# Attention in units of two heads, on even and odd query tokens

## The reference

```python
q_a, k_a, v_a, cx, cb, cc, q_m, gate_logits = split(rmsnorm(x) @ w_in)
# 12 attention heads of width 64: 3 groups x 4 slots
DIL_PATTERNS = ((128, 1), (512, 4), (2048, 16))   # (window, dilation) of a group
# query i attends the keys i + j*dilation with |j*dilation| <= window/2
s = where(valid, q . k / 8, -big)                  # inside each group
o_attn[slot] = sum over groups of softmax weights  # the groups are merged by their log-sum-exp
z_conv = cb * conv3(cc * cx)
# 4 memory heads of width 128 over 256 memory tokens
o_mem = softmax(q_m . k_m / sqrt(128)) @ v_m
x = x + (g0 * (o_attn @ w_proj_attn) + g1 * (z_conv @ w_proj_conv) + g2 * (o_mem @ w_proj_mem)) @ w_out
x = x + mixture_of_experts(rmsnorm(x))             # 32 experts, top 2 of one group of 8
```

## Time and profile before

| | |
|---|---|
| time, median of 3 runs | 2988.92 us (2987.07 to 2989.79) |
| span of the profiled execution | 2986.5 us, 2.4 us under the median |
| PE busy | 2817.0 us (94%) |
| DVE, ACT, POOL busy | 1155.4, 556.1, 621.8 us |
| chain that ended last | PE 86%, DMA 12%, DVE 1% |
| of that, slabs of the second block (L1561), experts' weights by DMA | 7%, 11% |
| attention stage, first scores to first `proj` | 2293.85 to 2459.64 us |

### The profile page before, as it was taken

How to read it: one execution, slowest core, us unless ns; L and a number is a source line. 1 busy time by engine, 2 the same in 40 slices (tenths; PEclk the granted TensorE clock), 3 DMA queues, 4 the chain that set the end, 5 groups by cost and what they waited for, 6 DMA issues and landing times.

```text
span 2986.5 us, 42182 instructions
## 1 busy us (share of the span) xinstructions
PE 2817.0 (94%) x18274; PEld 2423.2 (81%) x18274; DVE 1155.4 (39%) x2204; ACT 556.1 (19%) x856; POOL 621.8 (21%) x584
## 2 busy tenths in 40 slices
PE   8999999999999999999999999999999999866766
PEld 6888988889888899899988888889988888533433
DVE  3865235452433334745214344435355312210111
ACT  2101222124211101010033116210012330100000
POOL 0001411122121075068601210038800000000000
PEclk9999999999999999999999999999999999988878
DMA  9764543344443556764544444365433328899998
GB/s 406 297 263 163 175 150 134 121 141 171 140 141 127 196 199 229 272 219 166 183 147 143 139 153 143 130 224 170 165 135 130 105 91 351 381 432 430 430 430 371
DMA packets 74155, 641.62 MB, mean 215 GB/s; under 512 B 8304, under 2 KB 9584, under 8 KB 17648
## 3 DMA queue, kind: packets, MB, share of 16 engines
q1 hardware_dynamic: 71376, 631.55, 56.5%
q10 hardware_dynamic: 2592, 7.33, 0.6%
HBM read 637.80 MB, written 1.05 MB: 214 GB/s over the span
## 4 chain that ended last, share of the span: by engine, by line
PE 86%; DMA 12%; DVE 1%; issue 0%; ACT 0%; POOL 0%; SPq 0%; DVEq 0%; POOLq 0%; ACTq 0%
PE ps L1364 27%; PE ps L1340 20%; PE ps L1386 13%; DMA work<-in_w_moe 11%; PE ps L1561 7%; PE ps L1397 3%; PE ps L1591 2%; PE ps L1374 2%; PE ps L1145 2%; PE ps L1450 1%; PE ps L1167 1%; PE ps L1568 1%; PE ps L1272 1%; PE ps L1536 0%; PE ps L1539 0%; DMA ring<-in_w 0%
## 5 line engine op out<-in xcount | busy, mean ns | idle before, releaser
L2760 POOL TENSOR_TENSOR ring<-ring 128x512 f32<-128x512 f32 (+1 forms) x294 | 374.2, 1301 | 783.0 <-DMA ring<-in_w 315.7
L1364 PE MATMUL ps<-ring 128*128 128x256 f32 x2368 | 517.4, 380 | 0.6 <-ACT ring L1784 0.6
L1364 PEld LDWEIGHTS ps<-ring 128*128 128x128 f32 x2368 | 447.3, 190 | 63.2 <-issue 2.4
L2029 DVE TENSOR_TENSOR work<-work,ps 128x128 f32<-128x128 f32 (+3 forms) x534 | 185.6, 386 | 714.6 <-PE ps L1340 349.2
L1340 PE MATMUL ps<-work,ring 128*128 128x128 f32 x3312 | 385.8, 275 | 0.3 <-POOL work L2760 0.3
L1386 PE MATMUL ps<-work,ring 128*128 128x256 f32 x1760 | 385.5, 380 | 0.0
L1340 PEld LDWEIGHTS ps<-work,ring 128*128 128x128 f32 x3312 | 377.6, 192 | 0.5 <-POOL work L2760 0.5
L1386 PEld LDWEIGHTS ps<-work,ring 128*128 128x128 f32 x1760 | 332.5, 190 | 46.2 <-issue 2.1
L1364 PE MATMUL ps<-h,ring 128*128 128x256 f32 x1408 | 310.7, 382 | 6.5 <-ACT h L1784 2.9
L1364 PEld LDWEIGHTS ps<-h,ring 128*128 128x128 f32 x1408 | 265.8, 191 | 47.0 <-issue 5.7
L2029 DVE TENSOR_TENSOR work<-work 128x128 f32<-128x128 f32 (+4 forms) x566 | 261.6, 511 | 52.1 <-ACT eb L1812 24.9
(11 more groups left out here) (315 smaller groups left out, 2655.6 us busy)
## 6 DMA issues: line engine op xcount, KB each, us to landing
ring<-in_w SPq DMA_DIRECT2D x210, 1024.0 KB, 4.9
work<-in_w_moe SPq DMA_DIRECT2D x22, 4096.0 KB, 33.5
ring<-in_w_moe SPq DMA_DIRECT2D x22, 4096.0 KB, 33.4
ring<-in_w_in SPq DMA_DIRECT2D x80, 1024.0 KB, 4.9
work<-in_w_ada SPq DMA_DIRECT2D x40, 1024.0 KB, 6.1
ring<-in_w_ada SPq DMA_DIRECT2D x32, 1024.0 KB, 5.1
ring<-in_w SPq DMA_DIRECT2D x28, 768.0 KB, 4.2
ring<-in_w_out SPq DMA_DIRECT2D x16, 1024.0 KB, 5.1
```

What stands on the lines that cost most here:

```text
L1364: last = nc.tensor.matmul(ps[:, b, c * L:c * L + L], w[:, k * L + c * P:k * L + c * P + P], hs[cols][:, k, :], start=(k == 0), stop=(k == ...
L2029: return nc.vector.tensor_tensor(o, i0, i1, op)
L2760: return nc.gpsimd.tensor_tensor(o, i0, i1, ALU.subtract)
```

## The change

- There are 8 units, each with two neighbouring heads (`pair`). `t` is now a parity for form "a": even or odd query tokens (a stride of two in `q`, and in the normed `x` that is the stationary side of `va`, so that the values lie by parity too). Form "m" keeps its query tiles.
- Form "a", scores: the undilated group meets all 256 keys, the two dilated groups only the 128 of the query's parity. So a head's row of scores is 512 wide instead of 768. Head 0 of the pair uses array rows 0 to 63 and writes bank 4, head 1 uses rows 64 to 127 and writes bank 5.
- Maximum, sum and division are per head; ACT's exponential is two instructions of half the width.
- `turns`: 8 transposes ("a") or 4 ("m") and one wider copy. `mix`: 8 matmuls for "a", alternating between output rows 0 to 63 and 64 to 127, or 4 for "m". Its result goes to one of the four rotating banks; one ACT instruction copies both heads.
- Unit u has `scores` after slab 13 + 2u, `turns` after slab 14 + 2u, `mix` after slab 15 + 2u. The semaphore `un_out` is gone; `turns(u)` waits for the copy of the turns before (`un_pt`), and those who waited for 16 units wait for ACT's count after the last mix.
- Mask and `sc`, `pt` buffers are laid out for it.

```diff
-    for u in range(16):
-        side[u + 13].append(("scores", u))
-        side[u + 14].append(("turns", u))
-        side[u + 15].append(("mix", u))
+    for u in range(8):
+        side[2 * u + 13].append(("scores", u))
+        side[2 * u + 14].append(("turns", u))
+        side[2 * u + 15].append(("mix", u))
...
-        units = [("a", s, t) for s in range(4) for t in range(2)] + [("m", s, t) for s in range(4) for t in range(2)]
+        units = [(form, pair, t) for form in "am" for pair in range(2) for t in range(2)]
+        def parity(view, t):
+            return view.rearrange("p (u t) -> p t u", t=2)[:, t, :]
...
-                                last = nc.tensor.matmul(ps[:, b, t * L:t * L + L], hs[0][:, k, t * P:t * P + P],
+                                last = nc.tensor.matmul(ps[:, b, t * L:t * L + L], parity(hs[0][:, k, :], t),
...
                             for g in range(3):
-                                c = (g * 4 + slot) // 2
-                                last = nc.tensor.matmul(ps[:, 4 + g // 2, (g % 2) * L:(g % 2) * L + L],
-                                                        qk[r0:r0 + 64, c, t * P:t * P + P], qk[r0:r0 + 64, 6 + c, :],
-                                                        start=True, stop=True)
+                                c = 2 * g + pair
+                                for hh in range(2):
+                                    r = slice(64 * hh, 64 * hh + 64)
+                                    if g == 0:
+                                        dst, keys = ps[:, 4 + hh, 0:L].rearrange("p (t u) -> p t u", t=2), by_parity(qk[r, 6 + c, :])
+                                    else:
+                                        dst, keys = ps[:, 4 + hh, P + g * P:2 * P + g * P], parity(qk[r, 6 + c, :], t)
+                                    last = nc.tensor.matmul(dst, parity(qk[r, c, :], t), keys, start=True, stop=True,
+                                                            skip_group_check=True)
...
-                        nb = 6 if units[u][0] == "a" else 2
+                        nb = 8 if units[u][0] == "a" else 4
                         pe.wait_ge(un_pr, u + 1)
                         if u:
-                            pe.wait_ge(un_out, u)
+                            pe.wait_ge(un_pt, u)
...
+                        b = fresh()
...
+                            for j in range(4):
+                                g, tile = (0, j) if j < 2 else (j - 1, t)
+                                for hh in range(2):
+                                    hd = g * 4 + 2 * pair + hh
+                                    last = nc.tensor.matmul(ps[64 * hh:64 * hh + 64, b, 0:P], va[:, tile, hd * 64:hd * 64 + 64],
+                                                            pt[:, u % 2, hh * 512 + j * P:hh * 512 + j * P + P],
+                                                            start=(j == 0), stop=(j == 3), skip_group_check=True)
...
-                        nc.scalar.activation(sc[:, u % 2, 0:w], sc[:, u % 2, 0:w], ACT.Exp, bias=vms[:, u % 2:u % 2 + 1],
-                                             accum_out=vms[:, 2 + u % 2:3 + u % 2]).then_inc(un_ex, 1)
+                        for hh in range(2):
+                            last = nc.scalar.activation(sc[:, e, hh * w:hh * w + w], sc[:, e, hh * w:hh * w + w], ACT.Exp,
+                                                        bias=vms[:, 2 * e + hh:2 * e + hh + 1],
+                                                        accum_out=vms[:, 4 + 2 * e + hh:5 + 2 * e + hh])
+                        last.then_inc(un_ex, 1)
...
-                            nc.scalar.activation(oa[r, slot // 2, t * P:t * P + P], ps[r, 7, L:L + P], ACT.Copy
-                                                 ).then_inc(un_out, 1)
+                            nc.scalar.activation(parity(oa[:, pair, :], t), ps[:, b, 0:P], ACT.Copy).then_inc(ev_a, 1)
...
+                            own(stt(both, ps[:, 4:6, :], 64 ** -0.5, amask[:, t, :].unsqueeze(1).to_broadcast([P, 2, w]), mul, add))
...
+                        own(nc.vector.reciprocal(over, total))
+                        for hh in range(2):
+                            last = ts(sc[:, e, hh * w:hh * w + w], sc[:, e, hh * w:hh * w + w], over[:, hh:hh + 1], None, mul)
+                        last.then_inc(un_pr, 1)
```

More of the change, by code:

```diff
@@ L392, in __init__ @@
                 self.slabs += 1
-            if kind in ("gate", "up", "z", "wo", "mem", "msum", "xsum", "sum", "hsum", "in2", "proj", "out2") or (kind == "down" and stage[5] == 0):
+            if kind in ("gate", "up", "z", "wo", "mem", "msum", "xsum", "sum", "hsum", "in2", "mix", "proj", "out2") or (kind == "down" and stage[5] == 0):
                 assert groups < 4 or self.freed[groups - 4], (n, stage)
@@ L493, in __init__ @@
                 self.in2_at[stage[1:]] = self.a
+            elif kind == "mix":
+                self.a += 1
+                self.freed[self.group[n]] = ("a", self.a)
+                self.mixes_at = self.a
             elif kind == "hsum":
@@ L686, in build @@
         selw = shaped(mod[:].rearrange("p a b c -> p (a b c)")[0:N_EXP, 0:2 * P], 2, P)
-        sc = shaped(pmt[:, 0:2 * 3 * L], 2, 3 * L)
-        pt = shaped(glamask[:, 0:2 * 3 * L], 2, 3 * L)
+        sc = shaped(pmt[:], 2, 4 * L)
+        pt = shaped(glamask[:], 2, 4 * L)
         w_full = [sem(f"w_full{i}") for i in range(RING)]
@@ L1615, in first @@
                         u = stage[1]
-                        form, slot, t = units[u]
+                        form, pair, t = units[u]
                         if u == 0:
@@ L1649, in first @@
                         pe.wait_ge(un_pt, u + 1)
[L1650 to L1659, removed]
-                                                        xs[1][:, 4 + 2 * j + slot // 2, (slot % 2) * P:(slot % 2) * P + P],
-                                                        pt[:, u % 2, j * P:j * P + P], start=(j == 0), stop=(j == nb - 1))
+                        if form == "a":
+                            for j in range(4):
[5 more added lines that the diff above has]
+                                                            start=(j == 0), stop=(j == 3), skip_group_check=True)
+                        else:
+                            for hh in range(2):
+                                slot = 2 * pair + hh
+                                for j in range(2):
+                                    last = nc.tensor.matmul(ps[:, b, hh * P:hh * P + P],
+                                                            xs[1][:, 4 + 2 * j + slot // 2, (slot % 2) * P:(slot % 2) * P + P],
+                                                            pt[:, u % 2, hh * L + j * P:hh * L + j * P + P],
+                                                            start=(j == 0), stop=(j == 1), skip_group_check=True)
                         last.then_inc(un_o, 1)
@@ L1926, in first @@
                         u = stage[1]
[L1927 removed]
+                        form, pair, t = units[u]
+                        b = at.group[n] % 4
                         act.wait_ge(un_o, u + 1)
                         if form == "a":
[L1930 to L1934 removed]
+                            nc.scalar.activation(parity(oa[:, pair, :], t), ps[:, b, 0:P], ACT.Copy).then_inc(ev_a, 1)
+                        else:
+                            nc.scalar.activation(om[:, 2 * pair:2 * pair + 2, t * P:t * P + P],
+                                                 ps[:, b, 0:L].rearrange("p (s n) -> p s n", s=2), ACT.Copy).then_inc(ev_a, 1)
             act.dma_start(xs[1][:, :, :], a["ctx"]).then_inc(ctx_in, 16)
@@ L2522, in first @@
                         u = stage[1]
-                        form, slot, t = units[u]
+                        form, pair, t = units[u]
                         e = u % 2
-                        w = 3 * L if form == "a" else L
+                        w = 2 * L if form == "a" else L
                         if u == 0:
@@ L2848, in constants @@
         masks.append(np.where(ok, f(0), f(NEG)))
-    c["amask"] = np.ascontiguousarray(np.concatenate(masks, 1).astype(f).reshape(2, P, 3 * L).transpose(1, 0, 2))
+    near, fourth, sixteenth = masks
+    c["amask"] = np.stack([np.concatenate([near[t::2, 0::2], near[t::2, 1::2], fourth[t::2, t::2], sixteenth[t::2, t::2]], 1)
+                           for t in range(2)], 1).astype(f)
     c["desc"] = np.arange(8, 0, -1).astype(f)
```

39 lines of the change are left out of this document (20 added, 19 removed).

## The result

| | before | after |
|---|---|---|
| time, median | 2988.71 us (2987.07 to 2989.79, 4 runs) | 2969.51 us (2967.26 to 2970.20, 4 runs) |
| span of the profiled execution | 2986.5 us | 2965.7 us |
| first `scores` to first `proj` | 165.8 us | 146.1 us |
| first `proj` to the end | 526.9 us | 526.8 us |
| PE busy | 2817.0 us | 2796.8 us |

The ratio is 0.9933, 95% interval 0.9921 to 0.9945: the kernel is 19.2 us faster (forecast 20.2, time forecast 2968.7). Of the span's 20.8 us, 19.7 lie in the attention stage and 1.0 ahead of the first scores, where nothing was changed but the order of tokens in `va`. The stretch behind the stage is as long as before.

The account below looks back on a forecast made before the run. PE alone was taken to bound the attention stage, with later transfers started by PE. Attention on PE falls from 41.4 to 21.2 us (12.4 + 8.8), sparing 20.2: 2988.9 - 20.2 = 2968.7 us, range 2965.5 to 2976.5.

Parts of the forecast that it names:

- Rival (5): Experts' transfers start by something that didn't move, so spared time is not passed on: 2984 to 2989 us; chance 0.05.
- Scores "a": PE's scores block in four units: 1.06 us with two heads in row halves at once, 1.93 one after the other.
- Mix: PE's mix block of form "a": 16 passes in two column halves, 1.01 us, at worst 1.89.
- Transposes: PE's transposes block of form "a": 8 passes of 0.11 us plus 0.05, 0.93 us.
- Units "m": PE's four form "m" units: same products without the wait inside, 2.2 us each, 8.8 together, before 10.8.
- (1): Row halves don't overlap in scores, column halves in mix do: 3.5 us back, 2972.2 us; chance 0.10.
- (2): Neither scores' row halves nor mix's column halves overlap: 7.0 us back, 2975.7 us; chance 0.08.
- the variant with the loads in turn: Scores "a": the halves' weight loads go one after the other, 1.32 + 0.19 us; four units cost 1.8 us more.
- The chain: Softmax work between a unit's scores and transposes: 5.6 us, 5.8 with both ends; PE arrives after 6.91.
- Rival (3): PE waits at `turns` for a softmax of 8 us: 1 us in each of four units, 2972.7 us; chance 0.05.
- Strides: Queries, keys and `va` tokens read by PE with a stride of two floats: costed at nothing.
- Rival (4): Strided loads in `va` and scores "a" are slow: at f = 4, 3007.8 us; decides near f = 2.8; chance 0.04.

Follow-up runs that it names:

- x11: Changed kernel with both heads on the same array half and the parity-spared passes put back as repeats; stage 162.3 us against 146.1.
- x6: Changed kernel with the passes that the parity split spares put back as repeats, halves still side by side; stage 152.0 us, time 0.9955 of before.
- x3: Changed kernel with TensorE's operands read without the stride of two (output not the reference's); stage 145.9 us against 146.1.
- x10: Changed kernel with both heads of a form "a" pair on the same array half, same passes (output not the reference's); stage 153.3 us against 146.1.
- x7: Changed kernel with DVE's maximum of each form "a" unit taken twice; stage 146.1 us, as in the changed kernel.
- x8: Changed kernel with DVE's maximum of each form "a" unit taken four times; stage 158.8 us against 146.1, time 0.9979 of before.
- x4: Changed kernel with strided operands read at four floats instead of two (output not the reference's); stage 148.5 us against 146.1.

## Why the prediction was right

**PE bounds the stage and the rest follows it.** Right, and shown three ways: behind the stage it is 526.1 to 528.0 us in every kernel but x11, for stages from 146 to 159; x6 lost in the span what it lost in the stage; the first refill's issue moved by 20.7 us with the profile's 20.8, and from there to the end it is 434.2 us against 434.3. Rival (5) is out.

**The sum.** Forecast 21.2 us of attention on PE, measured 146.1 less 18 slabs of 6.91, 21.7: the stage is 0.5 us longer than forecast. Four terms make it up.

- Scores "a" were 1.13 instead of 1.06, 0.28 in four units; 0.05 of each 0.07 is the stride (x3 has 1.08).
- Mix was 1.01 forecast and 1.02 measured, 0.04 in all.
- Transposes took 0.87 instead of 0.93, 0.24 less in all. They now follow a slab, so no change of the array's form stands ahead of them.
- That change is paid elsewhere, and the forecast missed it. It counted one slab of 7.01 a unit, the one ahead of mix. Now a slab also stands directly behind the scores, and it takes 7.01 too: 0.4 in four units.

The trace of before shows this last cost in its first unit, the one whose scores have no transposes behind them (PE's timeline). The slab between two blocks of scores takes 7.10, with a change at both ends:

```profile
2295.34 7.17 PE L1561 MATMUL ps<-h,ring 128*128 128x256 f32 x32
2302.44 1.56 PE L1627 MATMUL ps<-work 64*128 64x256 f32 x6
```

Units "m" came to 0.89 + 0.87 + 0.44 = 2.2, as summed. The parts of the gain were given as 9 for scores left out, 7 for the halves and the rest (4.2) for fewer blocks; x11, x10 and the changed kernel give 9.0, 7.1 and 3.5, and some 2.1 of the 3.5 is the wait on bank 7. The forecast had this wait in its terms for "m" and the ends, but gave it to the blocks when it named the parts.

**From the span to the time.** The forecast set the time 2.4 us above the span, from one profiled span and the median of other executions, and took it as unchanged. Taken execution by execution, the time lies 1.8 us above its span before (13 executions, 1.8 to 1.9) and 3.2 to 3.3 above it after, and 1.8 again in x7 and x8. So about 1.4 us of what the span gained doesn't show in the time; why is open. That 2969.5 came within 0.8 us of 2968.7 is partly luck, since this term and the scatter ahead of the stage work against each other.

**The halves.** That rows 0 to 63 and 64 to 127 run side by side, loads and all, had no row in the trace of before. I took it from four column groups, and x10 against the changed kernel shows it: 0.92 us a block. Rivals (1) and (2), and the variant with the loads in turn (1.5), are out. The estimate from the Trainium skill, "TensorE: Matmul & The Clock Gate", section on packing small matmuls, of 0.3 us more a unit is not borne out: the difference was 0.07, most of it the stride.

**The wait.** The chain was forecast at 5.6 and is 5.34, since ACT's two halves take 1.55 from the first start to the division instead of 1.75. The cover was 1.5 us, forecast 1.1. Rival (3) is out, as PE doesn't wait. Its price was one for one, 1 us a unit for 1 us of wait. In x8 a wait of 2.28 us costs 3.2 a unit, and nearly all of the 0.9 on top stands where the clock was low; what a wait of 1 us would cost was not run.

**Strides.** They were costed at nothing; at a stride of two they cost 0.2 us. Rival (4) had a real mechanism: at four floats and at sixteen a load is slow, but not at two. Its price was wrong, though. x4 is near f = 2.2 (132 ns more on 0.11, an estimate), where the rival's sum gives 2.5 us for `va` and 8.1 for scores; measured were 1.6 and 2.4. It had the 48 loads of scores follow one another. If the halves load together, 24 times 0.24 instead of 3.5 us makes 2.3, which fits. By that its turning point is f = 3.4 and not 2.8, and x4 is far below either.

## What to carry to other kernels

Where PE alone sets the pace, read its blocks from start to start, split them into passes and a fixed part, and count every change of the array's form between neighbours (0.10 us on a slab here): the sum of this rewrite was good to half a microsecond. Two products of 64 rows, or of 64 output columns, made a block 1.8 times as fast when they alternated; put one after the other they kept less than half of what that saves. Before a step is moved closer to its user, add up the chain between them: up to the cover it was free (x7), beyond it PE's waits cost more than their length (x8: 12.7 us for 9.1 of waiting).

## What the runs showed of the hardware that I had not expected

- Two heads in turn in two halves still overlap in part: 1.70 and 1.51 us against 2.05 and 1.89 with one half only.
- A weight load of 128 columns with a stride of 16 bytes takes 329 ns, of 8 bytes 197, of 4 bytes 190; 64 bytes, 306.
- A gap of 2.1 us without a product brought the granted clock down in two of four cases; the blocks behind these two took 3.4 us longer, on top of 9.1 us of waiting.
- A change between the whole array and its halves costs 0.10 us on the slab beside it, on either side: 7.01 behind the scores and ahead of mix, 7.10 with both, 6.91 without.
- The time outside the profiled span isn't the same for all kernels: 1.8 us before, 3.2 to 3.3 after.
